# Moving loads, modulation chunks and attention's scratch in a two-block transformer kernel on one core

## The reference, cut to what matters

```
mod   = silu(c) @ w_mod[l] + b_mod[l]            # 6 rows of 1024, for c and for c_ctx
xn    = rms_norm(h, norm1_g[l]) * (1 + mod[1]) + mod[0]      # first norm, "modulated"
p     = xn @ w_in[l]                             # q, k, v, pool, conv (3), gates (3)
o     = diff_attn(q, [k, kc], [v, vc])           # 8 heads, keys of tokens and of context
mix   = (sig(g0) * norm(o) + sig(g1) * pool(p) * pool_scale + sig(g2) * conv(p)) @ w_out
h     = h + mod[2] * mix
xn2   = rms_norm(h, norm2_g[l]) * (1 + mod[4]) + mod[3]
h     = h + mod[5] * peer_ffn(xn2)               # top 16 of 16384 experts, 8 heads
```

## Time and profile before

| | |
|---|---|
| median of 3 runs | 4269.41 us (4262.23 to 4271.28) |
| the profiled execution | 4235.11 us, of which the span from first to last instruction is 4233.8 us |
| mean granted TensorE clock | 0.889 |
| busy share: PE, DVE, POOL, ACT | 77%, 47%, 37%, 9% |
| the chain that ended last: PE, DVE, DMA, POOL | 44%, 21%, 14%, 7% |
| moved by DMA | 1131.66 MB, 267 GB/s in the mean |

### The profile page before, as it was taken

The page is one execution under the profiler, slowest core; times in us unless marked ns, Lnnn a source line. Parts: engine busy times, 40 slices in busy tenths (PEclk is TensorE's granted clock), DMA queues, the critical chain, the costliest instruction groups (busy, mean ns, idle before and its releaser), DMA issues.

```text
span 4233.8 us, 28358 instructions
## 1 busy us (share of the span) xinstructions
PE 3250.0 (77%) x10162; PEld 1362.1 (32%) x10162; DVE 1972.7 (47%) x4408; ACT 377.1 (9%) x915; POOL 1547.0 (37%) x1608
## 2 busy tenths in 40 slices
PE   7999769777988886678788879777466665696786
PEld 1455335422542325222222223435011111144343
DVE  1023053777666634657666321344766666212132
ACT  1100041021000001000000010221000000002121
POOL 0010000455655662566666610002566666400000
PEclk9999989878999998889989989898788888898898
DMA  6234314888999996899999963126799999832312
GB/s 251 80 131 167 124 61 175 335 312 317 411 394 408 397 379 251 328 400 405 411 408 411 390 244 139 67 100 244 295 359 372 365 371 364 340 122 80 123 65 96
DMA packets 258713, 1131.66 MB, mean 267 GB/s; under 512 B 29600, under 2 KB 34720, under 8 KB 239372
## 3 DMA queue, kind: packets, MB, share of 16 engines
q0 software_dynamic: 221184, 805.40, 49.3%
q1 hardware_dynamic: 33964, 319.10, 19.4%
q10 hardware_dynamic: 3424, 5.34, 0.3%
HBM read 1123.34 MB, written 6.40 MB: 267 GB/s over the span
## 4 chain that ended last, share of the span: by engine, by line
PE 44%; DVE 21%; DMA 14%; POOL 7%; another core or an unknown queue 6%; issue 6%; ACT 2%; SPq 1%; DVEq 0%; ACTq 0%; POOLq 0%
PE ps L227 15%; DVE big L1944 9%; POOL big L1975 6%; DMA big<-in_u,xT 6%; PE ps L1804 5%; PE ps L528 4%; PE ps L1743 4%; DMA big<-in_v,xT 4%; PE ps L340 4%; DMA w<-in_w_in 2%; PE ps L540 1%; PE ps L468 1%; PE ps L1140 1%; PE ps L1280 1%
## 5 line engine op out<-in xcount | busy, mean ns | idle before, releaser
L1804 PE MATMUL ps<-big,bc 128*32 128x512 f32 x3072 | 1060.0, 691 | 348.0 <-DMA big<-in_v,xT 247.1
L1944 DVE CUSTOM_DVE_ANT_0 big<-big,ps 128x1024 f32<-128x1024 f32 x768 | 921.6, 1214 | 282.6 <-DMA big<-in_u,xT 222.0
L1975 POOL DMA_INDIRECT big<-in_u,xT x768 | 732.8, 954 | 616.2 <-issue 199.7
L1975 POOL DMA_INDIRECT big<-in_v,xT x768 | 731.3, 952 | 393.1 <-issue 202.9
L227 PE MATMUL ps<-w,xT 128*128 128x512 f32 x1408 | 614.5, 598 | 32.4 <-DMA w<-in_w_in 25.5
L1804 PEld LDWEIGHTS ps<-big,bc 128*32 128x32 f32 x3072 | 195.4, 118 | 1090.5 <-issue 559.8
L227 PEld LDWEIGHTS ps<-w,xT 128*128 128x128 f32 x1408 | 269.3, 192 | 372.7 <-issue 362.4
L340 PE MATMUL ps<-w,small 128*2 128x512 f32 x384 | 175.7, 612 | 48.7 <-DMA w<-in_w_mod 48.0
L528 PE MATMUL ps<-w,xT 128*128 128x512 f32 x384 | 176.6, 621 | 45.5 <-DMA w<-in_w_in 44.6
L408 POOL TENSOR_TENSOR small<-small 128x32 f32<-128x32 f32 (+1 forms) x8 | 33.2, 4155 | 453.5 <-DVE small L379 303.5
L1743 PE MATMUL ps<-tmp,w 128*128 128x256 f32 x768 | 178.9, 394 | 14.3 <-issue 11.6
(11 more groups left out here) (286 smaller groups left out, 3076.1 us busy)
## 6 DMA issues: line engine op xcount, KB each, us to landing
w<-in_w_in SPq DMA_DIRECT2D x58, 2048.0 KB
w<-in_w_mod SPq DMA_DIRECT2D x24, 2048.0 KB
w<-in_w_conv SPq DMA_DIRECT2D x24, 1536.0 KB
w<-in_peer_wq SPq DMA_DIRECT2D x12, 2048.0 KB
w<-in_w_out SPq DMA_DIRECT2D x10, 2048.0 KB
w<-in_conv_out_w SPq DMA_DIRECT2D x6, 2048.0 KB
big<-in_u,xT POOLq DMA_INDIRECT x768
big<-in_v,xT POOLq DMA_INDIRECT x768
```

The source lines that it names most:

```text
L1804: ins = pe.e.matmul(self.ps[32 * g:32 * g + 32, 2 + half, :], p["diag"][part % 2][:, 256 * g + 32 * m:256 * g + 32 * m + 32], p["ring"][:, ...
L1944: dve.inc(dve.e.tensor_tensor_reduce(out=row, in0=row, in1=p["xc"], scale=1.0, scalar=0.0, op0=ALU.mult, op1=ALU.add, accum_out=p["hid"][t ...
L1975: ins = pool.e.indirect_dma_start(p["ring"][:, slot, :], None, table, bass.IndirectOffsetOnAxis(index, 0))
```

## The change

- Attention's scratch moves from `w[s]` to `bc`: the lanes to rows 0 and 1, the sets to rows 2 to 5.
- Attention's gate weights are issued in `mix_sp` ahead of the wait for attention. The pool projection's weights of layer 0 are issued ahead of `convolved0`. In layer 1 band and scale are issued at its start and the pool gate's weights ahead of `convolved1`.
- The three first norms no longer use rows. DVE scales `h` by the reciprocal root alone (`rstd_dve`), PE turns it, one bank for each 128 columns (`modulated_pe`), and ACT (even banks) and DVE (odd banks) copy it to its place, multiplying by gain * (1 + scale) and adding the shift, which now are one number for each partition (`modulated`). `norm00` and `norm01` become one norm, `norm0`.
- For that, chunks 0 to 3 of each layer's modulation are turned from row to column: PE waits for ACT's copy, does four matmuls of 2 columns against the identity into bank 6, and ACT copies 8 columns to `mcol`. They are still stored to DRAM as well. DVE makes gain * (1 + scale) once for each layer (`mod_columns_dve`). The gain arrives as columns in one more small load at the start.
- Chunks move: in layer 0 only 0 to 3 stay in front; 4 stands behind k and v, 5 and 6 behind the convolution, 7, 8 and 9 behind the conv gate, 10 and 11 and chunks 0 and 1 of layer 1 behind the pool.

```diff
 def mods_pe / mods_act
             pe.inc(ins, "mod", l, c)
+            if c < 4:
+                pe.wait_ge(self.act, "mod copied", n)
+                if c:
+                    pe.wait_ge(self.act, "mod column", l, c - 1)
+                for j in range(4):
+                    ins = pe.e.matmul(self.ps[:, 6, 2 * j:2 * j + 2], self.mrow[at, j * P:(j + 1) * P], self.ident[at, at], start=True, stop=True)
+                pe.inc(ins, "mod turned", l, c)
...
+            if c < 4:
+                act.wait_ge(self.pe, "mod turned", l, c)
+                act.inc(act.e.copy(self.mcol[:, 32 * l + 8 * c:32 * l + 8 * c + 8], self.ps[:, 6, 0:8]), "mod column", l, c)
+    def rstd_dve(self, dve, name, tiles, dst):
...
+        dve.wait_ge(self.pool, name, "rstd")
+        for i, tile in enumerate(tiles):
+            dve.inc(dve.x.tensor_scalar(dst(i), self.h[:, tile, :], self.small[:, 8 + i:9 + i], None, ALU.mult), name, "scaled", i)
+    def modulated_pe(self, pe, name, src, n):
+        for k in range(KC):
+            for t in range(n):
+                if not k:
+                    pe.wait_ge(self.dve, name, "scaled", t)
+                ins = pe.e.transpose(self.ps[:, k, t * P:(t + 1) * P], src(t)[:, k * P:(k + 1) * P], self.ident[:, :])
+            pe.inc(ins, name, "turn", k)
+    def modulated(self, lane, name, l, streams, dst):
+        for k in range(lane is self.dve, KC, 2):
+            lane.wait_ge(self.pe, name, "turn", k)
+            lane.wait_ge(self.dve, "mod gain", l)
+            for i, s in enumerate(streams):
...
+                if lane is self.act:
+                    lane.inc(lane.e.activation(out, src, ACT.Identity, scale=gain, bias=shift))
+                else:
+                    lane.inc(lane.e.tensor_scalar(out, src, gain, shift, ALU.mult, ALU.add))
 def att_lane / att_set
-        return self.w[s][:, 0:1024].rearrange("p (a n) -> p a n", a=2)
+        return self.bc[:, s, :].rearrange("p (a n) -> p a n", a=2)
...
-        a = self.w[s]
-        return dict(e=a[:, 2048:3072].rearrange("p (i n) -> p i n", i=2), a=a[:, 3072:3584], aT=a[:, 3584:4096],
+        a = self.bc[:, 2 + 2 * s:4 + 2 * s, :].rearrange("p a b -> p (a b)")
+        return dict(e=a[:, 0:1024].rearrange("p (i n) -> p i n", i=2), a=a[:, 1024:1536], aT=a[:, 1536:2048],
 def layer0_sp
-        self.mods_stored(sp, 0, (0, 1))
-        for s in range(2):
-            self.norm_sp(sp, f"norm0{s}", range(3 * s, 3 * s + 3), self.d["norm1_g"][0:1, :], self.mod_row(0, s))
-        self.mods_sp(sp, 0, range(4, 8))
...
-        self.mods_sp(sp, 0, (8, 9))
+        self.mods_sp(sp, 0, (4,))
         self.conv_sp(sp, 0)
-        self.mods_sp(sp, 0, (10,))
+        self.mods_sp(sp, 0, (5, 6))
         self.gated_sp(sp, 0, 2, "conv")
-        self.mods_sp(sp, 0, (11,))
-        self.mods_sp(sp, 1, (0,))
+        self.mods_sp(sp, 0, (7, 8, 9))
+        self.linear_sp(sp, "pool0", 2, lambda c: self.w_cols(0, POOL_OFF + c * BANK), last=1)
         self.after(sp, "convolved0")
-        self.pool_sp(sp, 0, True)
-        self.mods_sp(sp, 1, (1,))
+        self.band_sp(sp, 0)
+        self.gated_sp(sp, 0, 1, "pool")
+        self.mods_sp(sp, 0, (10, 11))
+        self.mods_sp(sp, 1, (0, 1))
         self.after(sp, "pooled0")
 def mix_sp
+        self.gated_sp(sp, l, 0, None)
         self.after(sp, ("att", l))
...
-        self.gated_sp(sp, l, 0, None)
         self.residual_sp(sp, f"mix{l}", "w_out", l, 1)
 def layer0_act
-        self.norm_act(act, "norm00", [0, 1])
-        self.mods_act(act, 0, range(6))
...
+        self.norm_act(act, "norm0", [0, 1, 2, 3])
+        self.mods_act(act, 0, range(4))
+        self.modulated(act, "norm0", 0, (0, 1), self.xT)
 def layer1_sp
-        self.norm_sp(sp, "norm11", range(3, 6), self.d["norm1_g"][1:2, :], self.mod_row(1, 1))
+        self.band_sp(sp, 1)
...
-        self.after(sp, "convolved1")
-        self.pool_sp(sp, 1, False)
+        self.gated_sp(sp, 1, 1, "pool")
 def ahead_prep_sp
-        self.mods_stored(sp, 1, (0, 1))
-        self.norm_sp(sp, "norm10", (0, 1, 2), self.d["norm1_g"][1:2, :], self.mod_row(1, 0))
```

More of the change, by code:

```diff
@@ L178, in __init__ @@
         self.iota = self.small[:, 48:64]
+        self.mcol = self.small[:, 320:384]
     def side_lanes(self):
@@ L352, in mods_act, with mod_columns_dve @@
             self.mods_out[g].inc(act.e.dma_start(self.d["mods"][l][:, c * BANK:(c + 1) * BANK], self.mrow[at, :]), "mods", l, c)
+            if c < 4:
+                act.wait_ge(self.pe, "mod turned", l, c)
+                act.inc(act.e.copy(self.mcol[:, 32 * l + 8 * c:32 * l + 8 * c + 8], self.ps[:, 6, 0:8]), "mod column", l, c)
+    def mod_columns_dve(self, dve, l):
+        scale = self.mcol[:, 32 * l + 16:32 * l + 32].rearrange("p (k s) -> p k s", s=2)
+        gain = self.small[:, 416 + 8 * l:424 + 8 * l].unsqueeze(2).broadcast_to((P, KC, 2))
+        dve.wait_ge(self.bmod_in, "b_mod")
+        dve.wait_ge(self.act, "mod column", l, 3)
+        dve.inc(dve.x.scalar_tensor_tensor(out=scale, in0=scale, scalar=1.0, in1=gain, op0=ALU.add, op1=ALU.mult), "mod gain", l)
@@ new lines, in rstd_dve @@
+    def rstd_dve(self, dve, name, tiles, dst):
+        n = len(tiles)
+        s = self.small[:, 8:8 + n]
+        dve.wait_ge(self.act, name, "squares")
+        dve.inc(dve.x.tensor_scalar(s, s, 1.0 / D, EPS, ALU.mult, ALU.add), name, "mean")
+        dve.wait_ge(self.pool, name, "rstd")
[8 more added lines that the diff above has]
+            pe.inc(ins, name, "turn", k)
@@ L589, in pool_sp @@
         self.load_row(sp, 3, self.d["pool_scale"][l:l + 1, :], "pool scale", l)
-        if project:
-            self.linear_sp(sp, f"pool{l}", 2, lambda c: self.w_cols(l, POOL_OFF + c * BANK), last=1)
-        self.gated_sp(sp, l, 1, "pool")
     def pool_pe(self, pe, l, streams, project):
@@ L878, in layer0_pe @@
         pe.wait_ge(self.dve, "c silu")
-        self.mods_pe(pe, 0, range(8))
-        pe.wait_ge(self.dve, "norm01", "normed")
-        pe.wait_ge(self.act, "mod copied", 7)
-        self.transposed_pe(pe, "xT0", self.ba, 4)
-        pe.wait_ge(self.act, "xT0", "turned", 7)
+        self.mods_pe(pe, 0, range(4))
+        pe.wait_ge(self.act, "mod column", 0, 3)
+        self.modulated_pe(pe, "norm0", self.ba, 4)
+        self.modulated_ready(pe, "norm0")
         self.linear_pe(pe, "q0", self.lhs, [0, 1], 2, self.act)
@@ L978, in layer0_pool @@
     def layer0_pool(self, pool):
-        self.norm_pool(pool, "norm00", 2)
-        self.norm_pool(pool, "norm01", 2)
+        self.norm_pool(pool, "norm0", 4)
         for tile in range(4):
@@ L1036, in layer1_act @@
         self.mods_act(act, 1, range(4, 10))
-        self.transposed_act(act, "xT1", 2, self.xT[:, :, SEQ:2 * SEQ])
+        self.modulated(act, "norm11", 1, (1,), self.xT[:, :, SEQ:2 * SEQ])
         self.project_act(act, "kv1", [2, 3], self.kv_chunk, 4)
@@ L1051, in layer1_dve @@
         self.after(dve, "peer01")
-        self.norm_dve(dve, "norm11", [2, 3], lambda i: self.ba(2 + i), range(3, 6), True)
+        self.rstd_dve(dve, "norm11", [2, 3], lambda i: self.ba(2 + i))
+        self.modulated(dve, "norm11", 1, (1,), self.xT[:, :, SEQ:2 * SEQ])
         dve.wait_ge(self.ahead_in, "ahead in")
@@ L1095, in ahead_prep_pe @@
         self.after(pe, "peer00")
-        pe.wait_ge(self.dve, "norm10", "normed")
-        self.transposed_pe(pe, "aheadT", lambda i: self.merged[:, i, :], 2)
+        self.modulated_pe(pe, "norm10", lambda i: self.merged[:, i, :], 2)
         self.end(pe, "ahead ready")
@@ L1102, in ahead_prep_act @@
         self.norm_act(act, "norm10", [0, 1])
-        self.transposed_act(act, "aheadT", 2, self.aheadT())
+        self.modulated(act, "norm10", 1, (0,), self.aheadT())
         self.end(act, "ahead ready")
@@ L1107, in ahead_prep_dve @@
         self.after(dve, "peer00")
-        self.norm_dve(dve, "norm10", [0, 1], lambda i: self.merged[:, i, :], (0, 1, 2), True)
+        self.mod_columns_dve(dve, 1)
+        self.rstd_dve(dve, "norm10", [0, 1], lambda i: self.merged[:, i, :])
+        self.modulated(dve, "norm10", 1, (0,), self.aheadT())
         dve.wait_ge(self.taps_in, "taps", 1)
```

49 lines of the change are left out of this document (29 added, 20 removed).

## The result

| | before | after |
|---|---|---|
| median, beside each other (6 runs each) | 4265.82 us (4242.28 to 4285.10) | 4236.98 us (4229.60 to 4244.76) |
| the profiled execution | 4235.11 us | 4236.35 us (span 4235.0) |
| mean granted TensorE clock | 0.889 | 0.889 |

The ratio of the medians is 0.9933, 95% interval 0.9909 to 0.9957: 29 us faster, where 42 were forecast (0.9901, just outside the interval). The two profiled executions are equally long. That of before was 31 us faster than its median, that of after lies on its median. The difference lies in the expert stages, so I compare stage by stage. The table is made from the timeline of PE. A length runs from the first matmul of a stage to the first of the next; the convolution, attention, `peer00` and `peer01` end with their last matmul, and attention begins with its first L685 (L741 in the kernel after).

What follows compares the result with a forecast made beforehand. Transfers bound the three expert stages, PE with its waits for weights the rest of the first block. Terms sum to -42.3 us: profiled 4235.1 to 4192.8, median 4269.4 to 4227.1; range 4212 to 4242, with the first two rivals 4204 to 4246.

Steps and rivals of the forecast that it cites:

- The start: Layer 0 up to q: chunk 4's wait goes, squares, turns and a cold chunk come; -6.2 us with chunks put off.
- Ahead of the convolution: PE waits 6.1 us for the first conv chunk's load, plus 1.7 for a cold start: +7.8 us.
- Behind the convolution: Chunk 5 needs w[1], held by the last conv chunk: 7.3 us of load and 1.7 cold, +9.0 us.
- Barrier convolved0: PE's 12.46 us wait ahead of the pool projection shrinks to 0.7 and its cold start goes: -14.4 us.
- Behind the pool: Chunk 10 waits 3.7 us more for w[0], cold start as before, turns of chunks 0 and 1: +6.6 us.
- Attention's gate and chunks 2 and 3: Layer 0's gate loses its load wait and cold start, -16.5 us; turns of layer 1's chunks 2 and 3, +3.0.
- norm10: Norm without rows ahead of layer 0's expert stage: ready at 1607.5 us instead of 1617.8, -10.3 us.
- Layer 1: Smaller loads ahead of chunk 4, -0.5 us; band's wait goes, -5.0; attention's gate wait and cold start, -15.8.
- Pauses cost the clock: Rival, chance 0.12: each of eight turns sends PE to 1.2 GHz, 1.65 us each, 13 in all; 4240 us.
- Hidden waits: Rival, chance 0.10: the two new waits at the convolution, 16.8 us, are hidden; 4210 us.
- No early loads: Rival, chance 0.05: early gate loads don't come early as w[0] and w[1] aren't free; 32.3 us stay, 4259 us.
- Slower expert stages: Rival, chance 0.05: expert-stage fetches settle into another rhythm; from 1.7% the gain is gone, at 2.5% 4289 us.

Runs made afterwards that it cites:

- after_again: The changed kernel, unedited, profiled once more on another chip: 4110.63 us, one run.
- the second pair: The kernels before and after, both unedited, profiled once more on another chip: 4138.41 and 4110.63 us.
- parity: The changed kernel with modulation chunks 4 and 5 ahead of the convolution and chunk 6 behind it: 4090.7 us.
- att_only: The kernel before with only attention's scratch moved to `bc` and attention's gate weights issued ahead of attention: 4107.87 us, ratio to before 0.9935.
- defer: The changed kernel with each chunk's turn placed behind the matmuls of the next chunk, where one follows: 4098.0 us.
- both: The changed kernel with the edits of parity and defer together: 4076.72 us, ratio to before 0.9840; repeated as both_again on another chip: 4206.06 us, 0.9852.
- before_again: The kernel before, unedited, profiled once more on another chip: 4138.41 us, one run.
- norms_only: The changed kernel with scratch back in `w` and early loads undone, but attention's gate loads ahead of the four rows: 4137.8 us, ratio to before 1.0006.
- norms_in_order: The changed kernel with scratch back in `w` and early loads undone, attention's gate loads in their old order: 4154.54 us, ratio to before 1.0036.
- filled_after: The changed kernel with 16 unused identity transposes in PE's 2.80 us pause behind attention's gate, both layers: 4230.4 us, ratio to before 0.9915.

## Why the prediction was right, and where it missed

The direction, the mechanism and the range (4204 to 4246) held; the size was 42.3 us forecast, 29 measured. By the first pair of profiles, moved chunks put right at 7.90 us each:

- **The start**: -6.2 forecast, -3.6 measured. The terms for the squares (5.7, measured 5.85) and for the cold chunk held. The turn was 1.05 us and not 0.9, and 1.86 cold. The step "32 transposes in eight groups take 3.7" failed in this profile: 5.29, in part at the lower level. In after_again they took 3.72, and the chunk ahead of them 8.50 for 7.03.
- **Ahead of the convolution**: +7.8, measured +6.7, less 0.5 in the convolution. The wait was 6.68 for 6.1. The 1.7 of the cold start did not show, as DVE paces the stage. The 5.6 us estimated from the Trainium skill's page DMA: Bandwidth & Descriptors (section Anatomy of one DMA) lay further off; the page gives that fit for the path of GpSimd, and these loads are issued by SP.
- **Behind the convolution**: +9.0, measured +9.5 (7.48 of wait, 8.89 for the cold chunk).
- **Barrier convolved0**: -14.4, measured -14.5.
- **Behind the pool**: +6.6, measured +10.8. The step "its cold start is there as before" failed (9.73 for 8.72), and a further chunk fell to the lower level behind a pause of 0.67 us (8.72 for 7.03). The second half of the pool gate, behind the same wait as before, took 17.04 us for 15.62.
- **Attention's gate and chunks 2 and 3**: -16.5 and +3.0, together -13.5, measured -10.5 (-15.1 and +4.6). The wait and the cold start of the gate went as forecast (-14.9, 27.70 for 29.23); that PE and not DVE ends the gate held too. The step that failed is that the work behind the pause of 2.80 us stays warm, which I took from the earlier trace rows.
- **norm10**: -10.3, measured -10.5. (The terms of the chain add up to 1607.1, not 1607.5.)
- **Layer 1**: start and band -0.5 and -5.0, measured -0.5 and -5.1 (-4.2 up to the band matmuls and -0.9 in them, whose row is 8.68 us for 9.58). The sum was right and its reading wrong: that three rows less ahead of chunk 4 are worth 5 us was missed, and that the band, issued early, is loaded ahead of chunk 4 and costs 4.7 there was missed as well. The prediction costed the band's issue at nothing. Attention's gate: -15.8, measured -13.1, again for the clock.

Layer 0 as a whole: -10.7 forecast, -2.0 and, in the second pair, +0.2 measured. The change took 33 us out of layer 0 (start, barrier, gate) and put 31 in (ahead of and behind the convolution, behind the pool, ahead of the expert stage).

**The rivals.** *Pauses cost the clock* had 0.12 and 4240 us, and measured is 4237. It is right in part: not every turn sends PE to the lower level (in the profile of after three of the chunks that stand behind a turn take 7.03 us and two take 8.7), but the short pauses together cost 9.5 us of the 13 that are missing (42.3 less the 29.1 of the first pair): 1.6 at the start's transposes, 1.7 behind the pool, 1.6 and 1.6 at the two groups of transposes behind attention in layer 0, 0.5 and 2.5 at transposes and output matmul of layer 1. Of the 9.5, 4.9 lie behind turns, where that rival had put 13, and 4.6 behind the pause of 2.80, which it had not counted; so that its 4240 came nearer than the forecast is luck in part. The list is of chosen places: at the first twelve transposes of attention the two kernels differ as well, 2.79 for 1.50 us in layer 0 and 1.50 for 2.79 in layer 1. I set its chance by one window with clock 1.00 behind such a pause, which held in both layers of before, and did not ask whether the same pause could go otherwise elsewhere. The trace of before had cases of both kinds. "4.04 us is the shortest pause that cost something" was wrong by the earlier trace rows itself, where the chunk behind 3.90 us took 8.72, and the timeline of PE in before has shorter ones:

```profile
605.32 0.66 PE L707 MATMUL ps<-ident,w 128*128 128x128 f32 x4 [2.98 <-DVE w L793]
...
2717.45 2.79 PE L669 MATMUL ps<-ident,big 128*128 128x128 f32 x12 [2.65 <-DVE merged L580]
...
2764.98 1.12 PE L707 MATMUL ps<-ident,w 128*128 128x128 f32 x4 [2.98 <-DVE w L793]
```

The windows of before give these three stretches a granted clock of 1.00, 0.50 and 0.50: one pause of 2.98 us cost nothing, another of 2.98 at the same line did, and one of 2.65 did. The Trainium skill, TensorE: Matmul & The Clock Gate (section A second HAM failure mode), describes this swing by short idle times between groups of matmuls; the trace of after agrees at both pauses of 2.80 us and at one of 0.67 ahead of a chunk (8.72 us), and not at the other three of 0.67 ahead of one (7.03 each); that of before did not at its two of 2.80. *Hidden waits* falls by parity. *No early loads* falls by the 0.40 us at the gates. *Slower expert stages*, by 1% or more, falls by the second pair.

**What stays open**: why the pause of 2.80 us leaves the clock alone in the kernel before and not in the kernel after. It goes with what ran ahead of it. Where the gate began 0.40 us behind attention (two layers of after, after_again, att_only, parity, defer, both and both_again), the transposes were slowed in 14 of 14 places, to 2.35 to 3.53 us. Where the gate began behind 7.7 us of idle time or more (before, before_again, norms_only, norms_in_order), they took 1.94 us in 6 of 8 places and 3.33 and 3.54 in two. So in these runs a wait taken away ahead of the gate was mostly paid for in part behind it. Which property of the 30 us before the pause decides it, these runs don't tell. Whether attention's scratch in other rows changes attention itself was not tested by itself; its four lengths in the table, with either place, are 71.8 to 75.2 us, and the same kernel gave 71.8 and 75.2.

## What to carry to other kernels

When a load is moved, write down for each buffer who holds it and what is computed in the other one meanwhile: with two buffers in turn, one chunk more or less between two stages decided some 7 us of wait here, and so a group that lies between two users of the same pair should leave the turn of the buffers as it was. What is issued earlier stands ahead of something, and its price is to be sought there. And a large change should be cut into its parts before it is kept: here one moved line of loads and a new home for the scratch gave as much as the whole, and the elaborate part cost time until its order was put right.

## What was unexpected of the hardware

A turn, four float32 matmuls (8 passes that load 128 columns and stream 2) takes 1.05 us at the full clock and 1.86 at half: almost the 1.16 us of the same loads with 128 columns streamed. The weight loads of the two groups took 0.96 and 0.97 us by the timeline of PEld, so the load of the 128 columns is most of what is paid. A load of 1.5 MB ahead of the convolution let PE idle 6.40 to 6.68 us (six profiles), and one of 2 MB behind the convolution or behind the pool 7.36 to 7.97 us (eleven profiles), from the matmul that gives the buffer free. A pause of 0.67 us ended the full clock at one place (8.72 us for the chunk behind the first turn behind the pool, in six profiles of six: after, after_again, parity, norms_only, norms_in_order and filled_after). At others of the same length it did so in some profiles only: the fourth chunk of the start took 7.03 us in after and 8.50 in after_again, and the third 7.03 in after and 8.70 in filled_after. And the sets differ: `peer10`, in which DMA is busy 0.91 of the time, took 716 to 719 us in the sets on two chips and 792 to 807 in the others, for the kernels before and after alike; that is most of the 3% between the medians of one and the same kernel. Whether it is the chip or something else about the set, these runs don't tell.
